# State-space outputs: the order of the input and state products on TensorE, and the place of the second block copies in SyncE's list

## Chip, core and metric

The kernel runs on one core of a Trainium2 chip. The metric is the device time of one execution in microseconds (us), lower is better. Times inside an execution are counted from the start of the profiled span.

## What is computed

Two layers of a small transformer-like model over 256 tokens of width 1024. Layer 0 has a state-space mixer (the subject here), a gated linear unit (GLU) and a dense SwiGLU block; layer 1 has latent attention and a mixture of eight experts. In each layer six vectors ("modulation sections") come from one row vector and a 1024 x 6144 matrix. Cut to the part that matters:

```
mod = silu(c) @ w_ada[i] + b_ada[i]            # six sections of 1024
u = modulate(rms_norm(x), sh1, sc1)            # layer 0
h[t] = A h[t-1] + B u[t]                       # 64 groups, 64 complex states, 16 channels each
y[t] = Re(C h[t]) + d * u[t]
z = gelu(y); gl = z @ w_glu; out = gl[:, :1024] * sigmoid(gl[:, 1024:])
```

## The kernel before

Every engine has its own instruction list, written out by hand; semaphores order the lists against each other. The state-space part works on chunks of 8 tokens, so that 256 tokens are 32 chunks. For each of the 64 groups the output of a chunk is the sum of two products: an **input product** (`U`, the chunk's inputs, times `M`, a 128 x 128 block-triangular map of the inputs to the outputs of the same chunk) and a **state product** (`S`, the state at the chunk's start, times `O`). The groups are cut in two halves, `hf` 0 and 1. Outputs of half `hf` collect in PSUM banks `hf` and `hf + 2`.

`M` is made in three steps. ScalarE zeroes it (`zero_map`). TensorE computes `strips(part)` for part 0 and 1 and ScalarE copies them out (L1235, semaphore `strip_ok`). Then `m_blocks(eng, part, rows)` (L401 to L409) copies pieces of the strips into `M` by DMA: 32 DMAs a part, 16 on SyncE's queue (even rows) and 16 on ScalarE's (odd rows, L1271 and L1274), each adding 16 to `m_in[part]`. The input product of half `hf` waits for all 32 of part `hf`: `pe.wait_ge(m_in[hf], 16 * 32)`.

`outputs(hf)` (L723 to L752) is TensorE's list for one half:
- wait for `s_ok >= 2 * hf + 1`: VectorE has read the last of what the banks held before (L1755);
- L729: 16 matmuls that zero the two banks, from rows of `M` that are zero;
- wait for `m_in[hf]`, then L738: 64 matmuls, the input products, then `y_ps` + 1;
- wait for `s_ok >= 2 * hf + 2`: the states are ready (L1769), then L749: 128 matmuls, the state products, then `y_ps` + 1.

VectorE's `skip_term(0)` (L1775 transposes, L1779 adds) starts at `y_ps >= 3`, that is after the input products of half 1, since what it leads to (the GELU results) is written over `U`. `skip_term(1)` starts at `y_ps >= 4`. Between the two stand `split_to(1)` (L1521, the low part of the first GLU weight unit) and `mod_rows(4)`. ScalarE's GELUs and copies and VectorE's `z_lo` (L1786) follow, and TensorE's GLU (L797 on; its matmuls are recorded at L588 to L590) starts on the first of them.

`ada(n)` (L618, matmuls at L632) is one modulation unit: 16 matmuls on a 1 MB unit of `w_ada`. TensorE runs units 12 to 15, `strips(0)`, 16 to 19, `strips(1)`, 20 to 23, then `outputs(0)` and `outputs(1)`.

SyncE loads all weights in the order of `STREAM` into a ring of six 1 MB slots (`RING = 6`): entries 0 to 23 are the modulation units 0 to 23, entries 24 to 31 the eight GLU units (two DMAs each). Before entry `r` it waits until the user of entry `r - 6` has finished with the slot; for a modulation unit that is `ada_used`, raised by TensorE at the unit's last matmul. Entry 24 so waits for modulation unit 18, entry 25 for unit 19, entry 26 for unit 20. The block copies of part 0 and part 1 stand in this list behind the slot wait and ahead of the load of entries 21 and 24 (L439: `RING + 15`, `RING + 18`).

Of the kernel before, what the change touches and what calls it, by code (L numbers as in the profile page):

```python
# [31 lines left out]
NG, GH, NS, L = 64, 16, 64, 8  # L32
# [15 lines left out]
RING = 6  # L48
# [62 lines left out]
def program(nc, x_in, c_in, pos_in, norm_g, w_ada, b_ada, a_re, a_im, log_dt, b_re, b_im, c_re, c_im, d_in,  # L111
# [3 lines left out]
    with ctx:  # L115
# [285 lines left out]
        def m_blocks(eng, part, rows):  # L401

            eng.wait_ge(m_zero, 4)
            eng.wait_ge(strip_ok, 2 * part + 2)
            for i in rows:
                for c4 in range(4):
                    p0 = 32 * c4 + GH * (c4 % 2)
                    eng.dma_start(M[GH * i:GH * (i + 1), 32 * part + c4:32 * part + 32:4, GH * i:P],  # L408
                                  STRIPS[part][p0:p0 + GH, :, :, 0:(L - i) * GH].rearrange("p x b n -> p (x b) n")).then_inc(m_in[part], 16)  # L409


        @block.sync
        def _(sp):

            r0 = 0
            for src in (norm_g.rearrange("l i (t p) -> (l i t) p", p=P), d_in.rearrange("(t p) -> t p", p=P),
                        c_in.rearrange("a (t p) -> (a t) p", p=P), q_norm.rearrange("(t p) -> t p", p=P),
                        kv_norm.rearrange("(t p) -> t p", p=P)):
                n = src.shape[0]
                sp.dma_start(ROWS[r0:r0 + n, :], src).then_inc(rows_in, 16)  # L420
                r0 += n
            sp.dma_start(XN0[:, :, :], x_in[0].rearrange("(t p) n -> p t n", p=P)).then_inc(x_ld, 16)

            def load(slot, n):

                form, dims, src = unit_source(n)
                dst = RAW[:, slot, 0:unit_width(n)]
                dst = dst.rearrange(form, **dims) if dims else dst
                for g in range(dims.get("g", 1)):
                    part = (dst[:, :, g, :], src[:, :, g, :]) if "g" in dims else (dst, src)  # L430
                    sp.dma_start(*part).then_inc(raw_in[slot], 16)

            looped = 6 * MSTEPS - 1
            for r, (kind, n) in enumerate(STREAM[:RAW_OF_W[V_MOE + looped]]):
                if r >= RING:
                    k0, n0 = STREAM[r - RING]

                    sp.wait_ge(ada_used if k0 == "ada" else lo_done, n0 + 1)
                if r in (RING + 15, RING + 18):  # L439
                    m_blocks(sp, (r - RING - 15) // 3, range(0, L, 2))  # L440
                slot = r % RING
                if kind == "ada":
                    s, kk = divmod(n, 4)
                    src = w_ada[s // 6, 2 * kk * P:2 * (kk + 1) * P, (s % 6) * D:(s % 6 + 1) * D]
                    sp.dma_start(RAW[:, slot, :].rearrange("p (k n) -> p k n", k=2),
                                 src.rearrange("(k p) n -> p k n", p=P)).then_inc(raw_in[slot], 16)
                else:
                    load(slot, n)

            with sp.Fori(1, NE // 2) as i:  # L450
                for m in range(-1, looped):
                    sp.wait_ge(lo_done, moe_at(i, m - RING + 1))
                    slot = (RAW_OF_W[V_MOE] + m) % RING
                    tau, q = divmod(m + 1, 3)
                    j, s = divmod(tau - q // 2, MSTEPS)
                    if q < 2:
                        src = moe_in[bass.ds(i * 2 + j, 1), :, :].rearrange("o (k p) (g n) -> p (o k) g n", p=P, g=2)
                        dst = RAW[:, slot, :].rearrange("p (k g n) -> p k g n", k=4, g=2)
                        for g in range(2):
                            sp.dma_start(dst[:, :, g, :], src[:, 4 * q:4 * q + 4, g, s * FB:(s + 1) * FB])\  # L460
                                .then_inc(raw_in[slot], 16)
                    else:
                        src = moe_out[bass.ds(i * 2 + j, 1), s * FB:(s + 1) * FB, :].rearrange("o (k p) n -> p (o k) n", p=P)
                        sp.dma_start(RAW[:, slot, :].rearrange("p (k n) -> p k n", k=2), src).then_inc(raw_in[slot], 16)
            sp.wait_ge(lo_done, V_ALL - RING)
            load(RAW_OF_W[V_ALL - 1] % RING, V_ALL - 1)


            def pass_weights(e, k):
                w_e = moe_in[bass.ds(e, 1), :, :].rearrange("o (k p) (g n) -> p (o k) g n", p=P, g=2)  # L470
                wo_e = moe_out[bass.ds(e, 1), :, :].rearrange("o (s k p) n -> s p (o k) n", k=2, p=P)
                for s in range(MSTEPS):
                    if s == 0:
                        sp.wait_ge(v_hot, k * 3 + 1)
                    elif s >= 2:
                        sp.wait_ge(v_used, k * MSTEPS + s - 1)
                    for g in range(2):
                        sp.dma_start(VG[:, s % 2, :, g, :], w_e[:, :, g, s * FB:(s + 1) * FB])\
                            .then_inc(v_in[s % 2], 16)
                    sp.dma_start(VDN[:, s % 2, :, :], wo_e[s, :, :, :]).then_inc(v_in[s % 2], 16)  # L480

            most = most_crowded(sp)
            sp.wait_ge(lo_done, V_ALL)
            second_passes(sp, most, pass_weights)
# [98 lines left out]
        def _(pe):  # L583
# [116 lines left out]
            def strips(part):  # L700

                pe.wait_ge(o_ok, (4, 8)[part])
                if part:
                    pe.wait_ge(strip_ok, 2)
                for gq in range(4):
                    for c in range(2):
                        for g2 in range(2):
                            for c4 in range(4):
                                gi = 16 * part + 4 * gq + c4
                                half = slice(g2 * NS, (g2 + 1) * NS)  # L710
                                last = mm(PS[32 * c4:32 * c4 + 32, 6 + g2, gq * P:(gq + 1) * P],
                                          BB[half, c, gi - gi % 2:gi - gi % 2 + 2, :].rearrange("p g h -> p (g h)"),
                                          O[half, c, gi, 0:L, :].rearrange("p t h -> p (t h)"), start=c == 0, stop=c == 1)
                last.then_inc(strip_ps, 1)
# [5 lines left out]
                cols = PS[32 * c4:32 * c4 + 32, dt // 2, dt % 2 * SEQ:(dt % 2 + 1) * SEQ]  # L720
                return cols.rearrange("p (t a h) -> p a t h", t=L, a=2)[:, gg % 2, :, :]

            def outputs(hf):  # L723

                pe.wait_ge(s_ok, 2 * hf + 1)
                pe.wait_ge(m_zero, 4)
                for q in (hf, hf + 2):
                    for c4 in range(4):
                        mm(PS[32 * c4:32 * c4 + 32, q, :].rearrange("p (a n) -> p a n", a=16), M[96:P, 0, 0:32],  # L729
                           M[96:P, 0:16, 0:32], start=True, stop=False)  # L730
                pe.wait_ge(m_in[hf], 16 * 32)
                dts = (2 * hf, 2 * hf + 1)
                for dt in dts:
                    for a in range(2):
                        for g2 in range(2):
                            for c4 in range(4):
                                g = 8 * (dt + 4 * g2) + 2 * c4 + a
                                last = mm(y_tile(g), U[:, g, :], M[:, map_slot(g), :].rearrange("p (t h) -> p t h", t=L),  # L738
                                          start=False, stop=False)
                last.then_inc(y_ps, 1)  # L740
                pe.wait_ge(s_ok, 2 * hf + 2)
                for dt in dts:
                    for a in range(2):
                        for c in range(2):
                            for g2 in range(2):
                                for c4 in range(4):
                                    gi = 8 * dt + 2 * c4 + a
                                    half = slice(g2 * NS, (g2 + 1) * NS)
                                    last = mm(y_tile(g2 * GI + gi), S[half, c, gi, :],  # L749
                                              O[half, c, gi, 1:L + 1, :],  # L750
                                              start=False, stop=c == 1 and dt % 2 == 1 and a == 1)
                last.then_inc(y_ps, 1)  # L752
# [34 lines left out]
            for n in range(16, 20):  # L787
                ada(n)
            strips(1)
            for n in range(20, 24):  # L790
                ada(n)
            outputs(0)
            outputs(1)
            mod_columns(4)


# [1347 lines left out]
```

## Time and profile before

| | us |
|---|---|
| median of 3 runs | 1139.97 |
| lowest, highest | 1138.6, 1140.32 |
| the profiled execution | 1142.24 |
| its span in the trace | 1140.2 |
| TensorE busy | 1003.8 (88%) |
| VectorE busy | 825.0 (72%) |
| ScalarE busy | 622.0 (55%) |

The profiled execution is 2.04 us longer than its span, the part ahead of and behind the traced instructions, and 2.27 us above the median of the runs. The page of the profile gives busy shares over the whole span; this change touches a stretch of some 40 us, from 108 to 150 us. In the page's slices this is the fourth to the sixth of 40: TensorE is 6 to 8 tenths busy there and its granted clock 6 to 8 tenths of full.

### The profile page before, as it was taken

The page shows a single profiled execution, that of the slowest core. Times are in us where ns is not written, and L with a number is a line of the kernel's source. Part 1 is how long each engine was busy: PE and PEld are TensorE (multiplying, and loading weights), DVE is VectorE, ACT ScalarE, POOL GpSimd, SP SyncE. Part 2 cuts the span into 40 slices and gives each one's busy share as a digit, 9 for nine tenths or more (in the row PEclk, how much of TensorE's full clock was granted, in tenths as well). Part 3 has the DMA queues.
Part 4 walks back from the last instruction along what each step waited for, and adds up shares of the span by engine and source line. Part 5 has one row for each costly group of instructions (what it writes and reads, how often), then busy time and mean ns, then how long its engine had stood idle before and what let it go on. Part 6 is the DMA issues. An engine that isn't in the chain of part 4 may idle for free.

```text
span 1140.2 us, 17522 instructions
## 1 busy us (share of the span) xinstructions
PE 1003.8 (88%) x6576; PEld 823.5 (72%) x6577; DVE 825.0 (72%) x1119; ACT 622.0 (55%) x764; POOL 29.5 (3%) x73
## 2 busy tenths in 40 slices
PE   0776788899999987779868999999999999999993
PEld 0564367798989877556656888888888888888882
DVE  7899795444353547578338898898988888898884
ACT  4421164344342445465318776767777686767762
POOL 3000000000000000000100000000000000000000
PEclk9976789799999997889969999999999999999997
DMA  9847984296878775240307999999999999999951
GB/s 263 312 169 220 270 291 173 72 356 231 296 251 305 247 290 221 75 147 1 131 0 260 365 348 348 326 347 333 330 353 323 349 328 345 326 347 336 334 200 56
DMA packets 199107, 292.95 MB, mean 257 GB/s; under 512 B 18293, under 2 KB 164970, under 8 KB 198778
## 3 DMA queue, kind: packets, MB, share of 16 engines
q1 hardware_dynamic: 189114, 283.32, 72.2%
q10 hardware_dynamic: 8160, 5.85, 1.8%
q0 software_dynamic: 1760, 2.78, 1.1%
q8 instruction: 49, 0.80, 0.3%
q14 instruction: 24, 0.20, 0.0%
HBM read 287.39 MB, written 2.11 MB: 254 GB/s over the span
## 4 chain that ended last, share of the span: by engine, by line
issue 52%; PE 30%; DVE 9%; DMA 4%; ACT 2%; SPq 2%; POOL 0%; DVEq 0%; ACTq 0%; POOLq 0%
PE ps L588 8%; PE ps L589 7%; PE ps L590 7%; PE ps L632 2%; DMA raw<-in_w_ada 1%; SPq L408 1%; DMA mod_rows<-ada_wide 1%; DMA raw<-in_ffn_w_in 1%; PE ps L946 1%; PE ps L937 1%; ACT w_hi L1162 1%; PE ps L738 1%; PE ps L929 1%; PE ps L920 1%; PE ps L729 0%
## 5 line engine op out<-in xcount | busy, mean ns | idle before, releaser
L2032 DVE TENSOR_TENSOR w_lo<-raw,w_hi 128x2048 fp32r<-128x2048 f32 x166 | 375.1, 2288 | 64.9 <-ACT w_hi L1440 64.8
L1440 ACT ACTIVATE w_hi<-raw 128x2048 fp32r<-128x2048 f32 x166 | 311.3, 1909 | 0.3 <-issue 0.2
L1521 DVE TENSOR_TENSOR w_lo<-raw,w_hi 128x2048 fp32r<-128x2048 f32 (+3 forms) x55 | 122.6, 2248 | 109.6 <-ACT w_hi L1162 109.5
L588 PE MATMUL ps<-w_hi,xe_hi 128*128 128x512 f32 x448 | 179.6, 401 | 1.0 <-DVE w_lo L2032 0.7
L590 PE MATMUL ps<-w_hi,xe_lo 128*128 128x512 f32 x448 | 175.5, 392 | 0.0
L589 PE MATMUL ps<-w_lo,xe_hi 128*128 128x512 f32 x448 | 174.9, 390 | 0.0
L1162 ACT ACTIVATE w_hi<-raw 128x2048 fp32r<-128x2048 f32 (+3 forms) x55 | 101.8, 1878 | 97.0 <-DMA raw<-in_ffn_w_in 79.2
L588 PE MATMUL ps<-act_hi,w_hi 128*128 128x256 f32 x352 | 102.6, 292 | 1.0 <-DVE act_lo L1689 0.8
L589 PE MATMUL ps<-act_lo,w_hi 128*128 128x256 f32 x352 | 100.4, 285 | 0.0
L590 PE MATMUL ps<-act_hi,w_lo 128*128 128x256 f32 x352 | 100.3, 285 | 0.0
L590 PEld LDWEIGHTS ps<-w_hi,xe_lo 128*128 128x128 f32 x448 | 84.1, 188 | 17.8
L588 PEld LDWEIGHTS ps<-w_hi,xe_hi 128*128 128x128 f32 x448 | 84.2, 188 | 17.5 <-DVE w_lo L2032 1.1
L589 PEld LDWEIGHTS ps<-w_lo,xe_hi 128*128 128x128 f32 x448 | 84.4, 188 | 15.9
L1448 ACT ACTIVATE e_hi<-ps 128x256 fp32r<-128x256 f32 x56 | 21.5, 385 | 130.7 <-PE ps L1046 130.7
L588 PE MATMUL ps<-w_hi,e_hi 128*128 128x512 f32 x224 | 89.3, 399 | 1.4 <-DVE e_lo L2037 1.4
L590 PE MATMUL ps<-w_hi,e_lo 128*128 128x512 f32 x224 | 87.9, 392 | 0.0
L589 PE MATMUL ps<-w_lo,e_hi 128*128 128x512 f32 x224 | 87.9, 392 | 0.0
L588 PEld LDWEIGHTS ps<-act_hi,w_hi 128*128 128x128 f32 x352 | 68.0, 193 | 5.9 <-issue 4.8
L590 PEld LDWEIGHTS ps<-act_hi,w_lo 128*128 128x128 f32 x352 | 68.3, 194 | 0.0
L589 PEld LDWEIGHTS ps<-act_lo,w_hi 128*128 128x128 f32 x352 | 68.3, 194 | 0.0
L632 PE MATMUL ps<-raw,c_bcast 128*32 128x256 f32 x768 | 52.3, 421 | 5.2 <-DMA raw<-in_w_ada 5.2
L588 PEld LDWEIGHTS ps<-w_hi,e_hi 128*128 128x128 f32 x224 | 42.2, 188 | 10.8 <-issue 2.0
(396 smaller groups left out, 1586.6 us busy)
## 6 DMA issues: line engine op xcount, KB each, us to landing
raw<-in_moe_w_in SPq DMA_DIRECT2D x224, 512.0 KB, 5.4
raw<-in_moe_w_out SPq DMA_DIRECT2D x56, 1024.0 KB, 7.4
raw<-in_w_ada SPq DMA_DIRECT2D x48, 1024.0 KB, 9.4
raw<-in_ffn_w_in SPq DMA_DIRECT2D x44, 512.0 KB, 8.1
raw<-in_ffn_w_out SPq DMA_DIRECT2D x11, 1024.0 KB, 11.3
raw<-in_ssm_w_glu SPq DMA_DIRECT2D x16, 512.0 KB, 7.6
raw<-in_mla_w_o SPq DMA_DIRECT2D x4, 1024.0 KB, 7.8
raw<-in_mla_w_uq SPq DMA_DIRECT2D x3, 768.0 KB, 6.7
```

The lines of the kernel that those rows point to most:

```text
L408: eng.dma_start(M[GH * i:GH * (i + 1), 32 * part + c4:32 * part + 32:4, GH * i:P], STRIPS[part][p0:p0 + GH, :, :, 0:(L - i) * GH].rearrang ...
L588: mm(dst, st[0], mv[0], start=first, stop=False)
L589: mm(dst, st[0], mv[1], start=False, stop=False)
L590: return mm(dst, st[1], mv[0], start=False, stop=last)
L632: last = mm(PS[32 * c4:32 * c4 + 32, ada_bank(s), 0:256], CB[:, 2 * kk + k, :], RAW[:, RAW_OF_ADA[n] % RING, k * D + c4 * 256:k * D + (c4 ...
L738: last = mm(y_tile(g), U[:, g, :], M[:, map_slot(g), :].rearrange("p (t h) -> p t h", t=L), start=False, stop=False)
L920: last = tr(PS[0:QK, h % 2, (2 * i + tt) * P:(2 * i + tt + 1) * P], src[:, tt, h, :], IDENT[:, :])
L1162: af(HI[:, slot, 0:w], RAW[:, RAW_OF_W[v] % RING, 0:w], cp).then_inc(hi_done, 1)
L1440: af(HI[:, (V_MOE + m) % RING, :], RAW[:, (RAW_OF_W[V_MOE] + m) % RING, :], cp).then_inc(hi_done, 1)
L1448: af(EGH[:, tau % 2, :, :].rearrange("p a s -> p (a s)"), PS[:, 6, 0:2 * P], cp).then_inc(t_hi, 1)
L1521: tt_(LO[:, slot, 0:w], RAW[:, RAW_OF_W[v] % RING, 0:w], HI[:, slot, 0:w].bitcast(F32), ALU.subtract)\
L2032: tt_(LO[:, slot, :], RAW[:, (RAW_OF_W[V_MOE] + m) % RING, :], HI[:, slot, :].bitcast(F32), ALU.subtract)\
```

## The change

Two edits. TensorE's `outputs(hf)` is cut into `output_inputs(hf)` (waits for the banks and for `m_in`, L729 and L738 work) and `output_states(hf)` (wait for the states, L749 work). The order of TensorE's list after `strips(1)` was: modulation units 20 to 23, inputs 0, states 0, inputs 1, states 1. It becomes: inputs 0, modulation units 20 to 23, states 0, inputs 1, states 1. No instruction is added or removed. SyncE's block copies of part 1 move from ahead of the load of entry 24 to ahead of the load of entry 26.

```diff
-                if r in (RING + 15, RING + 18):
-                    m_blocks(sp, (r - RING - 15) // 3, range(0, L, 2))
+                if r in (RING + 15, RING + 20):
+                    m_blocks(sp, (r - RING - 15) // 5, range(0, L, 2))
...
-            def outputs(hf):
+            def output_inputs(hf):
 
                 pe.wait_ge(s_ok, 2 * hf + 1)
                 pe.wait_ge(m_zero, 4)
...
                 pe.wait_ge(m_in[hf], 16 * 32)
-                dts = (2 * hf, 2 * hf + 1)
-                for dt in dts:
+                for dt in (2 * hf, 2 * hf + 1):
...
                 last.then_inc(y_ps, 1)
+
+            def output_states(hf):
+
                 pe.wait_ge(s_ok, 2 * hf + 2)
-                for dt in dts:
+                for dt in (2 * hf, 2 * hf + 1):
...
             strips(1)
+            output_inputs(0)
             for n in range(20, 24):
                 ada(n)
-            outputs(0)
-            outputs(1)
+            output_states(0)
+            output_inputs(1)
+            output_states(1)
             mod_columns(4)
```

## Rows read from the trace of the kernel before

**Rows 1.** Page: the DMA queue that fetches instructions (packets, MB, share).
```profile
q8 instruction: 49, 0.80, 0.3%
```

**Rows 2.** The chain of waits, 105 to 151 us: start, duration (us), what.
```profile
108.50 12.82 DMA raw<-in_w_ada
...
121.36 1.93 PE ps L632 x16
123.30 3.57 PE ps L729 x16
126.86 3.44 PE ps L738 x64
130.31 1.96 PE ps L749 x128
132.27 1.85 PE ps L729 x16
134.12 0.56 PE ps L738 x11
134.67 2.22 issue
136.90 3.23 PE ps L738 x53
...
140.15 1.31 DVE s_y L1775 x2
...
145.95 1.22 DVE s_y L1775 x2
...
149.88 0.76 PE ps L588
```

**Rows 3.** Timeline of TensorE: start, duration, line, shapes, idle before and releaser.
```profile
108.18 3.67 PE L711 MATMUL ps<-s_out_map,s_bb 64*32 64x128 f32 x128 [4.41 <-DVE s_out_map L1706]
...
140.03 1.43 PE L749 MATMUL ps<-s_out_map,s_state 64*32 64x128 f32 x75
143.65 1.92 PE L749 MATMUL ps<-s_out_map,s_state 64*32 64x128 f32 x53 [2.18 <-issue]
```

**Rows 4.** Timeline of VectorE, 113 to 123 us.
```profile
114.90 0.69 DVE L1755 TENSOR_TENSOR s_tmp<-ps,s_phase 128x512 f32<-128x512 f32 x1
...
122.02 0.68 DVE L1769 TENSOR_TENSOR s_state<-s_state,s_tmp 128x496 f32<-128x496 f32 x1
```

**Rows 5.** Timeline of TensorE at 65 us: two modulation units at full clock.
```profile
65.74 1.93 PE L632 MATMUL ps<-raw,c_bcast 128*32 128x256 f32 x32
```

**Rows 6.** Timeline of SyncE's queue, 105 to 127 us: the DMA issues.
```profile
107.34 1.64 SPq L445 DMA_DIRECT2D raw<-in_w_ada  x3
113.25 12.58 SPq L408 DMA_DIRECT2D s_chunk_map<-s_strip_b  x16
```

**Rows 7.** SyncE's block copies of part 1: 119.4 to 120 us, then 125 to 125.8.
```profile
L408 SPq DMA_DIRECT2D s_chunk_map<-s_strip_b x2: 610/1184/1757, 118.9 to 119.5; - x2
...
L408 SPq DMA_DIRECT2D s_chunk_map<-s_strip_b x2: 604/608/612, 124.6 to 125.2; - x2
...
DMA to landing us min/median/max: 1.9/2.0/2.0
```

**Rows 8.** Timeline of ScalarE and its queue, 112 to 160 us.
```profile
113.25 12.96 ACTq L408 DMA_DIRECT2D s_chunk_map<-s_strip_b  x16
...
131.51 1.91 ACT L1162 ACTIVATE w_hi<-raw 128x2048 fp32r<-128x2048 f32 x1 [4.80 <-DMA raw<-in_ssm_w_glu]
...
150.64 9.11 ACT L1162 ACTIVATE w_hi<-raw 128x2048 fp32r<-128x2048 f32 x5
```

**Rows 9.** Busy time by stretch: PE, PEld, DVE, ACT, POOL, granted clock, DMA share, GB/s.
```profile
129.00:130.00 1.00, 1.00 (x25) 0.92 (x20) 0.97 (x3) 0.00 (x0) 0.00 (x0) 0.50 1.08 381
...
137.00:140.00 3.00, 3.00 (x53) 2.62 (x52) 0.00 (x0) 0.00 (x0) 0.00 (x0) 0.50 1.10 349
...
170.00:195.00 25.00, 25.00 (x112) 20.68 (x111) 11.12 (x9) 9.24 (x9) 0.00 (x0) 1.00 0.59 215
```

## The prediction

> **What bounds the kernel now.** I began with the page of the profile: a span of 1140.2 us, of which the change touches only some 40. So the totals say little, and I went to the chain of waits for 105 to 151 us, to see what ended last at each step. It runs so [rows 2]: the loads of the modulation weights until 121.36, modulation unit 23, then without a wait the zeroing, input and state products of half 0 to 132.27, the zeroing and 11 of the 64 input products of half 1, a stop of 2.22 us with no releaser ("issue"), the other 53 input products, and at 140.15 VectorE's transposes. From there VectorE works with hardly a stop (the second transposes at 145.95), and the GLU begins at 149.88. So the moment that counts is the end of the input products of half 1, which is `y_ps` 3: at 140.13 now. What follows up to the GLU is 9.7 us of VectorE's work, and the state products of half 1 run beside that.
>
> Then I asked whether a shift of that moment reaches the end. Behind 149.88 TensorE is busy without a break, 25.00 of 25.00 us in the stretch that I looked at, at full clock [rows 9], and the weight loads behind it are released by the consumers themselves, so they move with them. I take a shift of `y_ps` 3 as one for one in the total.
>
> **Part 1: the new order on TensorE.** The strips of part 1 end at 108.18 + 3.67 = 111.85 [rows 3]. The input products of half 0 then wait for L1755, which ends at 114.90 + 0.69 = 115.59 [rows 4]; I take 115.65. Their blocks of `M` (part 0) were issued by 107.34, when SyncE goes on to the next loads [rows 6], and a block lands 2.0 us after its issue [rows 7], so they are no limit. Zeroing and input products took 3.57 + 3.44 = 7.01 us at half clock [rows 2, 9]; they end at 122.66. Modulation unit 20 follows. A unit takes 1.93 us at half clock [rows 2] and 1.93 / 2 = 0.97 us at full clock [rows 5]. In the trace the clock rose at 130.0, 6.7 us after the same products had begun, and 8.6 us after TensorE's idle time had ended at 121.36 [rows 2, 9]; counted from 115.65 that is 122.4 or 124.3. I take half of each, 1.45 us: unit 20 ends at 124.1. Units 21 to 23 end at 127.0 to 129.9, the state products of half 0 (ready: L1769 ends at 122.70 [rows 4]) take 1.96 us more, the zeroing of half 1 1.85 us [rows 2]. So TensorE stands ready for the input products of half 1 at 131 to 134, where before it began them at 134.12. Taken alone this edit would be a gain: if the blocks were there, 64 products from 131 on end near 135, or 137 with the stop of 2.22 us, which is 3 to 5 us ahead of 140.13. The idle time of TensorE for modulation units 22 and 23 goes behind useful work.
>
> **Part 2: the block copies on SyncE.** Before, the 16 copies of part 1 went out at 113.25, when the strips were copied, took 12.58 us and so were over at 125.83 [rows 6]; the last landed 2.0 us after its issue [rows 7], near 127.2. They were covered with 7 us to spare. Moved to entry 26, they stand behind three things: the loads of entries 24 and 25 (four DMAs, free to go at about 109, right behind the three loads of 107.34 [rows 6]), and the slot wait of entry 26, which asks for the end of modulation unit 20. In the new order that unit stands behind the input products of half 0. So the copies start at 124.1 + 0.1 = 124.2, 11 us later than now. Behind them in SyncE's list are the loads of GLU units 2 to 5; in front of them in the sense of need stands TensorE at `m_in[1]`, and behind TensorE VectorE at `y_ps` 3.
>
> How long do the 16 take? The last ones, with nothing else new in the queues, took 0.61 us each and started 0.65 apart (124.6 to 125.2, rounded); one of the 16 took 1.76 us while loads were outstanding [rows 7]. The floor from the first start to the last is 15 x 0.65 = 9.75; as measured it was 125.2 - 113.25 = 11.95. By 126.2 ScalarE's own copies are over [rows 8] and the queue holds little besides, so I take a value near the floor, 10.4. The last starts at 134.6, lands at 136.6. TensorE, idle since 131 to 134, starts at 136.7, and after such an idle time its clock is down: the stop of 2.22 us was followed by 0.50 granted [rows 9]. The 64 products took 3.44 us at that clock, and 53 took 3.23, which makes 3.9 for 64 [rows 2]; I take 3.6. The stop of 2.22 us is not added: TensorE has waited for 3 us or more just before, and whatever the stop is, it most likely ends inside that wait. `y_ps` 3 falls at **140.3** against 140.13: +0.2 us.
>
> The state products of half 1 took from 140.03 to 145.57, with a stop of 2.18 us of their own [rows 3]; VectorE starts on their result at 145.95 [rows 2]. This stays as it is: VectorE's own work in between sets that start, with a margin of 0.3 us or so.
>
> **What else moves.** GLU unit 0 arrives some 10 us earlier, for nothing: ScalarE split it at 131.51 as soon as it landed [rows 8], and VectorE takes it up only between its two pairs of transposes, behind 140.15 [rows 2]. ScalarE's `wide(5)` now waits for unit 23, to 127.0 to 129.9, instead of 126.2 [rows 8]: it is followed by the same split and a wait for VectorE's first outputs, behind 140, so it costs nothing. GLU units 2 to 5 go out behind the copies, from 135.3: 4 MB at 349 GB/s [rows 9] are 12 us, so they are in by 149 to 150. ScalarE splits unit 1 from 150.64 and units 2 to 5 behind it until 159.75 [rows 8], one each 1.9 us: unit 2 (in at 140) has 12 us to spare and unit 5 (wanted at 158) 8. If that cover were gone, each us of delay would be a us of the GLU. Section 5 of the modulation, made from units 20 to 23, is used only behind the SwiGLU block.
>
> **Sum.** -4 to -5 us from the order on TensorE, +4 to +5 from the later copies, net +0.2 us in the span. The profiled execution (1142.24) would be 1142.4; its median answer is 1139.97 + 0.2 = **1140.2**.
>
> The bounds. Lowest: the clock is already full in the input products of half 0 (zeroing 1.85, products 64 / 11 x 0.56 = 3.3 [rows 2], unit 20 0.97): copies start at 121.9, 9.75 + 1.9 + 0.1, products 3.3: 137.0, that is -3.2. Highest: unit 20 at half clock, copies from 124.7, 11.95 + 2.0 + 0.1 + 3.9: 142.6, that is +2.5.
>
> **Rivals.**
> - *The copies are the new bound and cost more than the order gains* (the other side, slower). Place: TensorE at `m_in[1]`. Price: the highest sum above, +2.5 us, 1142.5. It decides from a last landing of 138.5 on (2.3 us behind 140.13 less the products). For it: one copy of part 1 took 1.76 us to issue while loads were outstanding [rows 7], and now 2 MB of GLU weights stand in the same queue right ahead. Against: 3 MB of modulation weights and 2 MB of these, from 108.5 on, are in at 123 by the 349 GB/s of a stretch without block copies [rows 9] and at 129 by the 3 MB in 12.82 us beside block copies [rows 2], so only the first few copies meet them.
> - *The stop of 2.22 us comes back in the input products of half 1, behind the wait.* Then `y_ps` 3 is at 142.5, +2.4 us, 1142.4. The two stops lie 53 + 75 = 128 matmuls apart [rows 2, 3]. I read them as instruction code that arrives late while weight loads fill the DMA engines; 49 packets of 0.80 MB in all are such fetches [rows 1], 16 KB each. If so, the wait hides the first. If the stop has another cause tied to its place in the list, it stays, since the count of matmuls ahead of it is unchanged. The Trainium skill speaks for the latter: "Runtime: NRT & Kernel Launch", section "Instruction fetch mechanics", has code streamed ahead in 16 KiB blocks and crossing a block "mostly hidden"; by that rule the stops are no fetches and the time would be 1142.4. The stops of this trace speak against the rule: they fall where the DMA engines' share is 1.08 to 1.10 [rows 9].
> - *The clock is full early and the copies go at their floor*: -3.2 us, 1136.8. For it: behind the stop of 2.22 us the clock came back within 3.2 us; from 140.03 on a state product takes 1.43 / 75 = 19 ns, near the 1.96 / 128 = 15 ns of full clock [rows 2, 3]. Against: with these same products it did not.
> - *The order gains its 4 to 5 us and the later copies cost nothing* (1135.5). This would need SyncE to pass entry 26 before unit 20 has run, which the slot wait forbids. I give it next to nothing.
>
> **How the numbers follow.** About 0.2% of this kernel, 2.3 us, is what a measurement can tell from no change. Forecast (shift of -1.5 to +2.2 us): 0.70. Copies slower than the order gains: 0.11. The stop returns: 0.08. Early clock: 0.08. Gain without cost: 0.03. Of the two slow rivals some end inside 2.3 us, and the runs themselves lie within 1.7 us of each other, so: faster 0.11, same 0.73, slower 0.16. The range takes in most of both slow rivals and the larger part of the early clock, which puts it at 1137.5 to 1143.0.
>
> **What would show it.** Right, if in the new profile: L738 of half 0 starts near 119.3 and unit 20 ends near 124; SyncE's 16 copies start then, not at 113; TensorE idles 3 us or more ahead of L738 of half 1, released by a DMA into the chunk map; the first stop is gone; VectorE's first transposes start within 1 us of 140.3; the GLU begins near 150. Wrong, if the copies start before unit 20 ends, if they take under 9 us or over 13, if the GLU's weight splits wait for a DMA, or if TensorE's GLU no longer starts 9.7 us behind the first transposes.

## The result, and the profile after

| | before | changed |
|---|---|---|
| median of the timed executions, us | 1139.69 (13) | 1142.2 (13) |
| lowest, highest | 1135.64, 1143.19 | 1138.96, 1145.83 |
| traced executions, us | 1142.24, 1140.06, 1141.24 | 1142.05, 1144.13 |

The change makes the kernel slower: ratio 1.003, 95% interval 1.0016 to 1.0044. The forecast was no change that can be told (1140.2 us, range 1137.5 to 1143.0); the time lies in the range, the sign was missed. The traced executions of before are three and those of the changed kernel two, since each kernel was traced again among the experiments.

The chain of waits of the changed kernel (start, duration, what) answers to [rows 2]:

```profile
114.21 3.63 PE ps L729 x16
117.84 3.36 PE ps L737 x64
121.20 0.91 PE ps L632 x16
122.14 0.60 SPq L408
...
133.51 0.60 SPq L408
134.16 1.92 DMA s_chunk_map<-s_strip_b
136.12 3.69 PE ps L737 x64
139.83 1.31 DVE s_y L1779 x2
...
145.64 1.22 DVE s_y L1779 x2
...
149.58 0.77 PE ps L588
```

L737 is the input product (L738 before), L751 the state product (L749 before). The chain has left the modulation weights and TensorE; from 122.14 to 136.12 it is SyncE's block copies and the last landing. The forecast had this form. SyncE's queue, its copies of part 1, and TensorE show the same from their sides (timeline of SyncE; copies of part 1 by line, with the landing of the 16; timeline of TensorE):

```profile
105.06 1.64 SPq L445 DMA_DIRECT2D raw<-in_w_ada  x3
106.74 8.82 SPq L431 DMA_DIRECT2D raw<-in_ssm_w_glu  x4
122.14 12.62 SPq L408 DMA_DIRECT2D s_chunk_map<-s_strip_b  x16
```

```profile
L408 SPq DMA_DIRECT2D s_chunk_map<-s_strip_b x16: 597/602/1681, 122.1 to 134.2; - x16
...
DMA to landing us min/median/max: 1.9/3.1/7.4
```

```profile
124.59 0.65 PE L751 MATMUL ps<-s_out_map,s_state 64*32 64x128 f32 x28
126.28 1.72 PE L751 MATMUL ps<-s_out_map,s_state 64*32 64x128 f32 x100 [1.04 <-issue]
...
136.12 3.64 PE L737 MATMUL ps<-s_chunk_map,s_u 128*32 128x128 f32 x64 [6.27 <-DMA s_chunk_map<-s_strip_b]
139.69 2.07 PE L751 MATMUL ps<-s_out_map,s_state 64*32 64x128 f32 x75
142.10 1.07 PE L751 MATMUL ps<-s_out_map,s_state 64*32 64x128 f32 x53 [0.34 <-issue]
```

TensorE stands idle 6.27 us for the last copy. The three 1 MB loads took 1.64 us to issue as before [rows 6], but the four that now stand ahead of the copies took 8.82, and the last of them landed only at 130.1 (issued at 111.8, 18.3 us to landing). The first copies, issued from 122.14 on, then needed up to 7.4 us to land where the last needed 1.9. The stop of 2.22 us in the input products of half 1 [rows 2] is gone, the 64 run in one piece.

Executions differ by 1 to 2 us before this stretch begins, so moments are compared from a fixed point from here on: VectorE's memset of the states, right behind its last output map (timeline of VectorE, the kernel before, then the changed one):

```profile
112.11 0.11 DVE L1745 MEMSET s_state<- 128x64 f32 x1
```

```profile
110.67 0.11 DVE L1749 MEMSET s_state<- 128x64 f32 x1
```

The time from there to VectorE's first transposes (the use of `y_ps` 3) and to the GLU's first matmul, for every traced execution, beside the timed ratio to the kernel before:

| kernel | to `y_ps` 3, us | to the GLU, us | ratio, 95% interval |
|---|---|---|---|
| before | 28.0, 26.2, 27.9 | 37.8, 35.9, 37.6 | 1 |
| changed | 29.2, 29.0 | 38.9, 38.8 | 1.003 (1.0016 to 1.0044) |
| order_only | 20.9, 22.3 | 30.7, 32.4 | 0.9977 (0.9966 to 0.9988) |
| copies_only | 28.3 | 38.0 | 1.0026 (1.0015 to 1.0037) |
| ahead_of_wait | 27.9 | 37.6 | 1.0022 (1.0012 to 1.0031) |
| late_no_loads | 27.2 | 37.0 | 1.0024 (1.0014 to 1.0034) |
| entry25 | 23.0 | 32.7 | 0.998 (0.9967 to 0.9992) |
| entry27 | 31.6 | 41.3 | 1.0067 (1.0046 to 1.0087) |
| units_in_gap | 23.1 | 32.9 | 0.9964 (0.9951 to 0.9978) |
| hold_from_25 | 22.8 | 32.6 | 0.9978 (0.9967 to 0.999) |
| order_and_hold | 20.9 | 30.6 | 0.996 (0.9946 to 0.9973) |
| glu_held | 22.2 | 35.9 | one execution, 1138.75 us |

Behind the GLU's first matmul the span goes on for 989.4 to 991.5 us in all 16 traces of the table, so what a kernel gains or loses lies ahead of that moment, to within 1 us or so either way.

### The profile page after: what moved, and what is told of

Its sections match the earlier page's. It is cut to its first block, busy times and chain, and to the rows that moved or that the text cites. A ratio compares the mean times of both kernels' runs of the same rounds, so it can differ in the third digit from the quotient of the medians.

```text
span 1139.9 us, 17522 instructions
## 1 busy us (share of the span) xinstructions
PE 999.2 (88%) x6576; PEld 819.7 (72%) x6577; DVE 824.3 (72%) x1119; ACT 621.7 (55%) x764; POOL 29.4 (3%) x73
## 4 chain that ended last, share of the span: by engine, by line
issue 52%; PE 30%; DVE 11%; DMA 3%; ACT 2%; SPq 1%; POOL 0%; DVEq 0%; ACTq 0%; POOLq 0%
PE ps L588 8%; PE ps L589 7%; PE ps L590 7%; PE ps L632 2%; SPq L408 1%; DMA raw<-in_ffn_w_in 1%; DMA mod_rows<-ada_wide 1%; PE ps L950 1%; PE ps L941 1%; ACT w_hi L1166 1%; PE ps L737 1%; PE ps L933 1%; PE ps L924 1%; DVE s_out_map L1705 1%; DVE s_out_map L1710 1%
## 5 line engine op out<-in xcount | busy, mean ns | idle before, releaser
L1452 ACT ACTIVATE e_hi<-ps 128x256 fp32r<-128x256 f32 x56 | 21.5, 385 | 130.7 <-PE ps L1050 130.7
```

What stands on the lines that cost most here:

```text
L1452: af(EGH[:, tau % 2, :, :].rearrange("p a s -> p (a s)"), PS[:, 6, 0:2 * P], cp).then_inc(t_hi, 1)
```

## The experiments

### The two edits apart

`order_only` is the changed kernel with SyncE's copies left where they were; `copies_only` is the kernel before with the copies moved.

```diff
-                if r in (RING + 15, RING + 20):
-                    m_blocks(sp, (r - RING - 15) // 5, range(0, L, 2))
+                if r in (RING + 15, RING + 18):
+                    m_blocks(sp, (r - RING - 15) // 3, range(0, L, 2))
```

> The new order on TensorE, the block copies of part 1 left ahead of entry 24. Theory 1 (the moved copies eat what the order gains): the copies start near 112 us, land by 126, TensorE goes from the state products of half 0 straight into the input products of half 1 near 130 us, y_ps 3 comes 4 to 6 us earlier against VectorE's first memset of the states than in the kernel before, and the time is 1134 to 1136.5 us (before 1139.7). Theory 2 (the loss is made elsewhere, by the new order itself or behind the GLU's start): no gain, 1139 to 1143 us.

> The old order on TensorE, the block copies of part 1 moved to entry 26. Theory 1: unit 20 stands right behind the strips in this order and ends near 113 us, so the copies start at 115 to 117 us, behind the four loads, and land by 130; TensorE asks for them at 134. Time as before, 1139 to 1140.5 us. Theory 2 (the move alone costs, through the load order or the queue): 1141.5 us or more.

Measured: the order alone 1135.9 us (median of 12), ratio 0.9977; the copies alone 1141.71, ratio 1.0026. SyncE's queue, then TensorE, of `order_only`:

```profile
111.70 11.79 SPq L408 DMA_DIRECT2D s_chunk_map<-s_strip_b  x16
```

```profile
128.14 0.62 PE L737 MATMUL ps<-s_chunk_map,s_u 128*32 128x128 f32 x11
129.36 1.73 PE L737 MATMUL ps<-s_chunk_map,s_u 128*32 128x128 f32 x53 [0.59 <-issue]
131.56 1.32 PE L751 MATMUL ps<-s_out_map,s_state 64*32 64x128 f32 x75 [0.48 <-DVE s_state L1773]
136.11 1.07 PE L751 MATMUL ps<-s_out_map,s_state 64*32 64x128 f32 x53 [3.22 <-issue]
```

No wait for a copy is left in it; `y_ps` 3 comes at 20.9 us, just where VectorE ends its own work on the states of half 1 (131.56 is released by it). So the order alone gains, by 2.6 us of ratio in the timed executions and more in the traces, and the move of the copies costs more than that: 1142.2 - 1135.9 = 6.3 us (6.0 by the ratios).

`copies_only` missed the expectation of theory 1. Its copies started at 116.17, as expected, but did not land by 130 (SyncE's queue; TensorE; the copies' landings; busy time by stretch with granted clock, DMA share, GB/s at the end):

```profile
106.85 9.21 SPq L431 DMA_DIRECT2D raw<-in_ssm_w_glu  x4
116.17 14.30 SPq L408 DMA_DIRECT2D s_chunk_map<-s_strip_b  x16
```

```profile
135.27 3.64 PE L738 MATMUL ps<-s_chunk_map,s_u 128*32 128x128 f32 x64 [5.50 <-DMA s_chunk_map<-s_strip_b]
```

```profile
L408 SPq DMA_DIRECT2D s_chunk_map<-s_strip_b x16: 599/688/2192, 116.2 to 129.5; - x16
...
DMA to landing us min/median/max: 5.3/8.4/9.5
```

```profile
126.00:130.00 4.00, 3.77 (x144) 2.05 (x140) 3.93 (x6) 2.56 (x3) 0.00 (x0) 1.00 1.45 114
130.00:134.00 4.00, 0.00 (x0) 0.00 (x0) 1.56 (x3) 0.00 (x0) 0.00 (x0) 0.81 1.03 159
```

Each copy took 5.3 to 9.5 us to land. From 126 to 130 us the DMA engines are full (share 1.45) while they move only 114 GB/s: the small pieces of the block copies and the weights share them. The last copy lands 5.8 us after SyncE's last start at 129.5. So the 2 MB ahead delay the copies inside the DMA engines, not only at their issue. ScalarE's 16 copies, which no edit moves and which go out from 111.8 on (113.3 in before), show it too: 6.4 to 9.8 us to land here and 6.6 to 8.6 in the changed kernel, 1.9 to 5.8 in the kernel before. Before, with the same number of copies and 3 MB of modulation weights, they were through by 127.

### Which of the two delays: the slot wait or the loads ahead

`ahead_of_wait` leaves the two loads ahead of the copies but takes the copies out from behind the wait for unit 20; `late_no_loads` does the opposite. Both edits are against the changed kernel.

```diff
+                if r == RING + 20:
+                    m_blocks(sp, 1, range(0, L, 2))
                 if r >= RING:
                     k0, n0 = STREAM[r - RING]
                     sp.wait_ge(ada_used if k0 == "ada" else lo_done, n0 + 1)
-                if r in (RING + 15, RING + 20):
-                    m_blocks(sp, (r - RING - 15) // 5, range(0, L, 2))
+                if r == RING + 15:
+                    m_blocks(sp, 0, range(0, L, 2))
```

```diff
-                if r in (RING + 15, RING + 20):
-                    m_blocks(sp, (r - RING - 15) // 5, range(0, L, 2))
+                if r in (RING + 15, RING + 18):
+                    if r == RING + 18:
+                        sp.wait_ge(ada_used, 21)
+                    m_blocks(sp, (r - RING - 15) // 3, range(0, L, 2))
```

> The changed kernel, but SyncE's copies of part 1 stand ahead of the slot wait of entry 26, not behind it; the loads of entries 24 and 25 stay ahead of them. Theory 1 (the wait for modulation unit 20 is what makes them late): the copies start near 115.6 us, right behind the four loads, last landing near 130; y_ps 3 near 134 to 136 and a time of 1135 to 1137.5 us. Rival (the queue is the cause: 2 MB of loads ahead in the same queue): the copies take 16 us or more instead of 12.6, and the time stays at 1140 us or more.

> The changed kernel's order on TensorE; SyncE's copies of part 1 wait for modulation unit 20 as there, but the loads of entries 24 and 25 stand behind them, not ahead. So they start as late (121 to 122.5 us) with nothing ahead in the queue. If the late start alone makes them late: last landing 133.5 to 135.5, y_ps 3 28 to 29 us from the memset, time 1140.5 to 1142. If the 2 MB ahead of them are the whole cause: the copies land at once, issue in 10 us, y_ps 3 at 26 or less, time 1137 to 1139.5.

Measured: 1141.72 us (ratio 1.0022) and 1141.48 us (1.0024). Either cause alone makes nearly the whole loss. In `ahead_of_wait` the copies start 5.0 us from the memset (11.5 in the changed kernel), and still TensorE is released only at 135.67 (SyncE's queue, then TensorE). They did not take the 16 us to issue that the rival expected, they landed late:

```profile
116.57 13.66 SPq L408 DMA_DIRECT2D s_chunk_map<-s_strip_b  x16
```

```profile
135.67 3.64 PE L739 MATMUL ps<-s_chunk_map,s_u 128*32 128x128 f32 x64 [4.69 <-DMA s_chunk_map<-s_strip_b]
```

In `late_no_loads` they start at 122.14, 11.4 us from the memset (11.5 in the changed kernel), and with nothing ahead the 16 starts span 10.3 us (12.0 there) and land within 2.8 (7.4 there):

```profile
122.14 10.85 SPq L408 DMA_DIRECT2D s_chunk_map<-s_strip_b  x16
```

```profile
L408 SPq DMA_DIRECT2D s_chunk_map<-s_strip_b x16: 597/602/1037, 122.1 to 132.4; - x16
...
DMA to landing us min/median/max: 1.9/2.2/2.8
```

TensorE still waits, and is released at 134.34:

```profile
134.34 3.58 PE L739 MATMUL ps<-s_chunk_map,s_u 128*32 128x128 f32 x64 [5.79 <-DMA s_chunk_map<-s_strip_b]
```

From the memset, `y_ps` 3 is at 21.6 us with neither (mean of the two traces of `order_only`), 27.2 with the late start alone, 27.9 with the loads alone and 29.1 with both (mean of two). The two do not add up: each of them makes the copies land after TensorE needs them, and the second only 1 to 2 us later still. Theory 1 named the slot wait alone and was half right; "the queue is the cause" was half right as well.

### The dose

`entry25` puts the copies ahead of entry 25 (`RING + 19`), `entry27` ahead of entry 27 (`RING + 21`), with the divisor to match.

> The changed kernel with SyncE's copies of part 1 ahead of entry 25: one weight unit (1 MB) ahead of them instead of two, and no wait for unit 20. If what stands ahead in the DMA queues sets the last landing, it falls half way between the kernel with none ahead (TensorE did not wait, 128) and with two ahead (135 to 136): 130 to 133 us, y_ps 3 at 23 to 26 us from the memset, time 1136.5 to 1140. If only the slot wait mattered: as with none ahead, y_ps 3 at 21 and 1136.

> The changed kernel with the copies of part 1 one entry later, at 27: behind modulation unit 21 and two more load issues. Theory 1: the start of the copies moves from 122.1 to 123.5 to 125.5 us, and the time with it by 1.5 to 3.5 us against the changed kernel (1142.2), so 1143.7 to 1145.7. Theory 2 (copies are no bound): unchanged at 1142.2.

Measured: 1137.36 us (0.998) and 1145.24 us (1.0067). With 1 MB ahead TensorE does not wait for a copy, with 3 MB and unit 21 ahead it waits 8.6 us (what TensorE waited for, 120 to 140 us of `entry25`, 125 to 145 of `entry27`):

```profile
PE ps L751 <- issue: 2.3, 2, 2.2
PE ps L737 <- issue: 1.2, 1, 1.2
```

```profile
PE ps L737 <- DMA s_chunk_map<-s_strip_b: 8.6, 1, 8.6
```

From entry 24 to 25, 26 and 27 the medians are 1135.9, 1137.4, 1142.2, 1145.2. `entry27` was expected within this band, for both reasons together; `entry25` came nearer to the kernel with none ahead than "half way": its ratio (0.998) can't be told from that of `order_only` (0.9977), and no copy is waited for in its trace. That `y_ps` 3 comes at 23.0 and not at 20.9 or 22.3 is the stop of 1.2 us and the 53 products behind it, which took 3.10 us where they took 1.73 in `order_only`. So the first 1 MB ahead of the copies cost nothing that shows, and the loss begins with the second.

### Is the missing time in the stop?

The first traced execution of before was 2.5 us above its median, and the forecast rested on it. Theory 3: its stop of 2.22 us is not usual.

> The kernel before once more, for its trace. The one traced execution of it took 1142.24 us, 2.5 us over its median of 1139.69, and had a stop of 2.22 us inside the input products of half 1, ahead of y_ps 3. Theory 3: that stop (instruction code that comes late) is short or missing in most executions, so this one takes 1138 to 1140.5 us, with y_ps 3 nearer than 28.05 us to VectorE's first memset of the states: 26 to 27. Rival: the stop is always there at about 2 us and the 2.5 us lie in other stretches, y_ps 3 at 28.0.

> As before_2, one more execution: theory 3 wants the time to follow the length of that stop, 26 to 27 us from the memset to y_ps 3 and 1138 to 1140.5 us; the rival wants 28.0 with any time.

Measured 1140.06 and 1141.24 us, the first within the band of theory 3, the second above it. But the stop is there in both (TensorE, `before_2`, then `before_3`):

```profile
134.10 2.86 PE L738 MATMUL ps<-s_chunk_map,s_u 128*32 128x128 f32 x53 [2.11 <-issue]
```

```profile
135.45 3.21 PE L738 MATMUL ps<-s_chunk_map,s_u 128*32 128x128 f32 x53 [2.10 <-issue]
```

So theory 3 fell; what differs is when the last modulation weights land and the products of half 0 begin: `y_ps` 3 is at 28.0, 26.2 and 27.9. The repeats of the other two kernels:

> The new order alone once more, for its trace. Its first traced execution took 1133.0 us against a median of 1135.9 in the timed ones, with y_ps 3 at 20.87 us from the memset. If the trace was a lucky one: y_ps 3 at 22 to 25 here and 1134 to 1138 us. If that moment is steady: 20.9 to 21.5 and 1132.5 to 1135.

> The changed kernel once more, for its trace: copies of part 1 from 11.3 to 12 us after the memset, 12 to 13 us for the 16 of them, y_ps 3 at 28.8 to 30 us, GLU at 38.5 to 40, 1141 to 1144 us. A value of 27.5 or less would say that the delay against the kernel before was chance.

Measured 1135.55 and 1144.13 us. `y_ps` 3 is at 22.3 in the one, as the first expectation had it (the first trace of `order_only` was a lucky one), and 29.0 in the other, as expected there. The changed kernel's two traces agree here to 0.2 us; means are 27.4 for before and 29.1 for the changed kernel, **+1.7 us**.

What the stop is, `glu_held` tells: the kernel before, with one wait added ahead of entry 24, so that no GLU weight is under way during the products; from 126 us on the DMA engines are empty.

```diff
+                if r == RING + 18:
+                    sp.wait_ge(y_ps, 3)
```

> The kernel before, but SyncE waits for y_ps 3 ahead of the load of entry 24, so that no GLU weight is on its way while TensorE runs the products of both halves. If the stop of 2.1 us after 11 of the 64 input products of half 1 is instruction code that comes late under the weight loads: the stop shrinks to under 1 us and y_ps 3 comes at 26 to 26.7 us from the memset (28.05, 26.2 and 27.9 in the three traces of before). If it belongs to its place in the list: 2.1 us as before. The GLU's weights arrive 14 us later, so the GLU starts later and the time is 1142 to 1152 us either way; the time is not the point.

Measured: 1138.75 us, one execution. The stop is gone (TensorE; then busy time by stretch, DMA share 0.01 to 0.03):

```profile
130.96 1.95 PE L740 MATMUL ps<-s_chunk_map,s_u 128*32 128x128 f32 x64
132.84 1.32 PE L751 MATMUL ps<-s_out_map,s_state 64*32 64x128 f32 x75
134.50 1.07 PE L751 MATMUL ps<-s_out_map,s_state 64*32 64x128 f32 x53 [0.33 <-issue]
```

```profile
126.00:130.00 4.00, 4.00 (x170) 2.93 (x164) 3.93 (x6) 0.00 (x0) 0.00 (x0) 0.91 0.03 6
130.00:134.00 4.00, 4.00 (x151) 2.88 (x144) 2.65 (x5) 0.00 (x0) 0.00 (x0) 1.00 0.01 4
```

The same instructions at the same place no longer stop once no weight is on its way. `y_ps` 3 came at 22.2, earlier than the 26 expected: the products of half 1 began at 20.2 us from the memset (20.5 to 21.9 in before), and all 64 ran at a granted 1.00 in 1.95 us, where in the three traces of before the 53 behind the stop took 2.9 to 3.2 (granted 0.50 [rows 9]). So a stop costs its own 2.1 us and 1 us or more of clock.

The stops' places fit code that arrives in blocks: the changed kernel stops after 28 of the 128 state products of half 0; 100 + 16 + 11 = 127 matmuls on stands the 11th input product of half 1, where the kernel before and `order_only` stop; and 53 + 75 = 128 on is the next. The traces also hold the fetches themselves. The DMA queue "q8 instruction" [rows 1] carried one packet of 16 KB near each stop. It shows in before at 134.4 and 141.0 us, in `glu_held` at 128.2 and 132.1 (DMA queues in windows of 0.1 us from these moments):

```profile
q8 instruction: 1, 0.02, 67.4%
q8 instruction: 1, 0.02, 71.2%
```

```profile
q8 instruction: 1, 0.02, 89.7%
q8 instruction: 1, 0.02, 59.3%
```

Set against TensorE's list, with a block ending after 28 of the state products of half 0 and the next one after 11 input products of half 1:

| trace | TensorE enters a block, us | packet, us later | TensorE goes on after the stop at the block's end, us behind the packet |
|---|---|---|---|
| before | 130.7, 136.9 | 3.7, 4.1 | 2.5, 2.65 |
| before_2 | 127.9, 134.1 | 3.8, 4.1 | 2.4, 2.65 |
| before_3 | 129.4, 135.45 | 3.5, 4.15 | 2.55, 2.6 |
| glu_held | 127.6, 131.6 | 0.6, 0.5 | no stop, 2.4 |

The packet for the next block came 0.5 to 0.6 us after TensorE entered a block where the DMA engines were idle, and 3.5 to 4.15 us after it where weights filled them; from the packet to TensorE's next matmul it was 2.4 to 2.65 us wherever it stopped (2.3 to 3.0 in the traces of the other kernels). TensorE ran from 130.7 to the end of that block, 134.67, in 4.0 us: 3.7 + 2.5 - 4.0 = 2.2 us is the stop of before, and 0.6 + 2.4 = 3.0 us is less than 4.0, so `glu_held` has none there. That TensorE's entry into a block is what asks for the next one is inferred from these times. The stop is late code, and what makes it late is the wait of one packet among the weight loads.

The execution was also faster than expected (1142 to 1152). ScalarE split GLU unit 0 some 8 us later from the memset, which put the GLU 13.7 us behind `y_ps` 3 (9.7 in before), but its first matmul still came at 35.9 and the GLU itself was no longer than in before (53.1 us from its start to TensorE's next product, 53.0 to 53.5 there). So in this one execution the late weights cost less than the stops.

### Is the stop there in timed executions?

Over most kernels of the table the timed difference (the ratio's, of 1139 us) is near the traced `y_ps` 3 less 25.2, to within 1.3 us: -2.3 us at 23.0 (`entry25`), +2.7 at 27.2 (`late_no_loads`), +3.0 at 28.3 (`copies_only`), +7.6 at 31.6 (`entry27`). Two kernels stand further below this line. Before itself, at 27.4, would be at +2.2 and is at 0; `units_in_gap`, at 23.1 in its one trace, would be at -2.1 and is at -4.1. Theory 4: its stop is missing when it is timed. `hold_from_25` is before with the wait one entry later, so that GLU unit 0 is in time; `order_and_hold` is the same wait in `order_only`.

```diff
+                if r == RING + 19:
+                    sp.wait_ge(y_ps, 3)
```

> The kernel before, but SyncE waits for y_ps 3 ahead of the load of entry 25: GLU unit 0 comes as before, units 1 to 5 go out some 12 us later, so that no weight load is under way in the products of half 1. In the trace both stops of TensorE shrink to under 0.7 us, y_ps 3 comes at 24.5 to 26 us from the memset (27.4 on average in before), the GLU starts 9.7 us behind it and no weight split waits. If the stop of 2.1 us is in the timed executions of before too: ratio 0.9975 to 0.9990 (1136 to 1138 us). If it is missing there (the kernel before is then faster than its traces): ratio 0.9990 to 1.0008.

> The new order on TensorE, the copies ahead of entry 24, and the wait for y_ps 3 ahead of entry 25. In the trace: no stop over 0.7 us, y_ps 3 where VectorE's work on the states ends, 20.9 us from the memset, second transposes at 26.6, GLU at 30.6. If the stops are in the timed executions of the new order (0.6 to 1.5 and 3.2 to 3.8 us in its traces): ratio 0.995 to 0.9968, 1 to 2 us below the new order alone (0.9977). If not: 0.997 to 0.9985, as that.

Measured: 1136.03 us (ratio 0.9978, 12 executions) and 1134.2 us (0.996, 5). TensorE of `hold_from_25`:

```profile
131.26 2.16 PE L740 MATMUL ps<-s_chunk_map,s_u 128*32 128x128 f32 x64
133.34 1.32 PE L751 MATMUL ps<-s_out_map,s_state 64*32 64x128 f32 x75
135.70 1.07 PE L751 MATMUL ps<-s_out_map,s_state 64*32 64x128 f32 x53 [1.03 <-issue]
```

A gain of 0.22% (interval 0.10 to 0.33), 2.5 us, is in the band expected if the stop is in timed executions, so theory 4 fell too. How far it fills the gap is open. In the traces the hold brings `y_ps` 3 forward by 4.6 us (27.4 to 22.8, the stop and the clock behind it; 24.5 to 26 was expected, and the second stop, 1.03 us, is longer than the 0.7 expected). The held weights give 0.8 us of it back, against the expectation that no split waits: ScalarE waits 3.01 and 2.73 us for GLU units 4 and 5, and the way from the GLU's start to TensorE's next product behind it is 54.0 us against 53.0 to 53.5 in before. At that product the traces are 3.7 us apart (90.3 us from the memset in before on average, 86.6 with the hold), at the upper edge of the 1.1 to 3.8 us of the timed executions.

`order_and_hold` has the best time of all, and its ratio lies in the band for stops that are in the timed executions. No copy is waited for, one stop of 0.55 us is left, and `y_ps` 3 comes where VectorE's own work ends (TensorE):

```profile
129.24 1.72 PE L739 MATMUL ps<-s_chunk_map,s_u 128*32 128x128 f32 x53 [0.55 <-issue]
131.50 2.26 PE L753 MATMUL ps<-s_out_map,s_state 64*32 64x128 f32 x128 [0.54 <-DVE s_state L1775]
```

The interval of its ratio overlaps that of the new order alone (0.9966 to 0.9988), so what the hold adds to the new order is not shown.

### A filler that was not needed

`units_in_gap` is `order_only` with modulation units 20 and 21 ahead of `output_inputs(0)`.

```diff
+            ada(20)
+            ada(21)
             output_inputs(0)
-            for n in range(20, 24):
-                ada(n)
+            ada(22)
+            ada(23)
```

> The new order with the copies ahead of entry 24, and modulation units 20 and 21 ahead of the input products of half 0, in the 3.8 us in which TensorE waits there for VectorE. TensorE would be ready with the input products of half 1 about 2 us earlier (19 us from the memset), but VectorE's own work on the states of half 1 ends at 20.9. If VectorE bounds the new order already: y_ps 3's use stays at 20.9 to 21.2, time 1134 to 1136, no more than 1 us from the new order alone. If TensorE is late in most timed executions (median 1135.9 against 1133.0 traced): 1132.5 to 1134.5.

Measured: 1135.51 us, ratio 0.9964 from 5 executions, within the interval of `order_only`. In the trace the copies themselves were the limit this time (16 in 14.03 us, then a wait of 3.57), `y_ps` 3 at 23.1:

```profile
129.84 3.64 PE L737 MATMUL ps<-s_chunk_map,s_u 128*32 128x128 f32 x64 [3.57 <-DMA s_chunk_map<-s_strip_b]
```

The time is in the band of the first expectation, `y_ps` 3 is not; the run decides nothing between them, and shows that even at entry 24 the copies can be late once TensorE is ready earlier.

## Why the prediction was wrong

**What held.** The part that bounds, and the shift one for one to within 1 us or so: `entry27`, 2.5 us later at `y_ps` 3 than the changed kernel, was 3.0 us slower by the medians. The chain through SyncE's copies, started by unit 20 (forecast 124.2 us, which is 12.1 from the memset; measured 122.14, 11.5). TensorE ready long before (129.85). The clock at half rate for the 64 products (3.64 us; 3.6 taken). The stop hidden by the wait, and its cause, late code: the packets of `glu_held` and of the three traces of before show it. The rival on this point leaned on the Trainium skill ("Runtime: NRT & Kernel Launch", "Instruction fetch mechanics": the cost of crossing a block is "mostly hidden"). Here it was hidden with idle DMA engines (0 and 0.33 us) and not under full weight loads (2.1 to 2.3 us at every stop of before). The GLU's weights in time, 9.7 us from `y_ps` 3 to the GLU.

**What failed, first: the term of the copies.** I took 10.4 us from the first start to the last, near the floor, since "the queue holds little besides", though the row of before said 11.95. Measured: 134.16 - 122.14 = 12.0 in the changed kernel. The 10.4 is right only when nothing is ahead: 10.3 in `late_no_loads`. The step behind it was that the 2 MB would be in by 123 to 129, "so only the first few copies meet them". They were in at 130.1, so that of the 16 starts of 12.0 us the first 8 us met them: the first copies landed after 7.4 us, and four loads had taken 8.82 us to issue. This is +1.6 us; the earlier start of the copies gives back 0.6 (the granted clock was 1.00 from 121 on, for the whole of unit 20, where I had taken half of each level); in all +1.0 against my sum (29.1 for the 28.2 that 140.3 stands for). I had the right mechanism as the first rival (the copies "cost more than the order gains") and gave it 0.11.

**Second: one traced execution as the measure of before.** 140.13 us is 28.0 from the memset, and the mean of three traces is 27.4. The products of half 0 start behind landings of 1 MB loads, 14.7, 13.1 and 15.1 us from the memset, a spread of 2 us between executions; the new chain (29.2, 29.0) doesn't scatter so in its two traces. That is +0.7 us. I knew that the traced execution stood 2.3 us above the median and wrote the forecast as 1142.4 for its own kind; carrying the +0.2 over to the median was the step that lost the sign. With the two, the traces give +1.7 us at `y_ps` 3, just below the interval of the ratio (1.8 to 5.0 us).

One more term stood at nothing in the sum. Behind its wait the changed kernel runs the first 5.1 to 5.3 us of the GLU at half clock (granted 0.50), where before was at full clock after 3.5 to 4.5. From the memset to TensorE's next product behind the GLU it is 92.5 us on average in the changed kernel and 90.3 in before, +2.2 us. At the end of the span the difference is 1.7 again, so this term isn't shown to reach the end.

**Third: the two halves of the sum.** I had the order's gain at 3 to 5 us and the copies' cost at 4 to 5. Measured in timed executions: 3.1 us (1139.0 to 1135.9) and 6.3 us. The traces give 5.8 and 7.5. Also the +4 to +5 us of the later copies was priced as if the slot wait made the cost; `ahead_of_wait` and `copies_only` show that the loads ahead alone make it, so the move would have cost 3 us even without the new order. And the lowest sum took 3.3 us for 64 input products at full clock, from 11 products in 0.56 us; 64 took 1.95 us at a granted 1.00 in `glu_held`, so that bound stood too high.

**What stays open.** The timed executions differ by 2.5 us (medians) or 3.4 (the ratio), the traces by 1.9 as a whole and by 2.2 to the GLU's end. Before is faster when timed (medians of 1138.7 to 1139.7) than in its three traces (mean 1141.2; of its 90 timed executions 19 took as long as the fastest of the three), the changed kernel is less so (1142.2, 1143.1), and `order_only` is slower when timed (1135.9, traces 1134.3). The stop is in the timed executions, but its full size there is not shown. Three and two traces may be too few.

## What to carry to other kernels

Moving small DMAs behind large loads in one queue delays them twice, at the issue and in the engines, and the delay is worth looking up in the landing times of a stretch where both kinds were under way. A prefetched weight can cost more than its own arrival gains: here it held up the engine's own code. When a reorder makes an engine ready earlier, whatever had slack against it becomes the bound, so it should stay as early as it was: here the reorder alone gained what both edits together lost. A net that is the small difference of two terms of 4 to 6 us is no forecast of "the same"; its spread is that of the terms.

## What the runs showed of the hardware

- TensorE's list stopped for 2.1 to 2.3 us twice, 128 matmuls apart, under full weight loads in all three traces of before, and for 0 and 0.33 us with the DMA engines at 0.01 to 0.03 of their share. The 16 KB packet with the next code came 3.5 to 4.15 us after TensorE had entered a block in the one case and 0.5 to 0.6 in the other. Holding back 5 MB of weights over a stretch of dense small matmuls gained 0.22% by itself.
- Behind the first stop of before the granted clock was 0.50 [rows 9]: 53 products took 2.9 to 3.2 us in its three traces, where all 64 took 1.95 at 1.00 in `glu_held`.
- With block copies of small pieces and weight loads together the DMA engines show a share of 1.45 at 114 GB/s (`copies_only`); with weights alone 1.10 at 349 [rows 9].
- Four 512 KB loads took 8.82 us to issue behind three of 1 MB in the changed kernel, the last two 3.4 and 3.8 us each; two of them, in `entry25`, took 1.70. So SyncE itself was held up at the third and fourth.
